# Dealing the second half of the value spread and the state readings out in turn on TensorE, in a hybrid decoder step

## The reference

```
cm_new = decay * cm + w_end * outer(vc, kc)        # state update: decay, then a rank-1 term
num    = ... cm, qc ...                            # the state read by the query
```

## Time and profile before

| | us |
|---|---|
| runs of the kernel before, median of 3 (lowest, highest) | 2174.12 (2170.67, 2176.59) |
| profiled execution | 2170.06 |
| its span, first to last instruction | 2168.2 |
| TensorE matmul busy in the span | 2078.0 (96%) |
| mean granted TensorE clock | 0.957 of full speed |

### The profile page before, as it was taken

The page is one execution under the profiler, slowest core; times in us unless marked ns, Lnnn a source line. Parts: engine busy times, 40 slices in busy tenths (PEclk is TensorE's granted clock), DMA queues, the critical chain, the costliest instruction groups (busy, mean ns, idle before and its releaser), DMA issues.

```text
span 2168.2 us, 39328 instructions
## 1 busy us (share of the span) xinstructions
PE 2078.0 (96%) x16091; PEld 1968.4 (91%) x16091; DVE 1221.4 (56%) x1836; ACT 977.0 (45%) x1594; POOL 285.8 (13%) x288
## 2 busy tenths in 40 slices
PE   7999999998999989999999997999999999999997
PEld 6998878996899979988799976999999999999997
DVE  6556445543556665655355425566566656665665
ACT  4444234444454544441344433454454545454544
POOL 0891122000000007921220000000000000000000
PEclk9999779999999999997799997999999999999999
DMA  7553224458446355532244484454546454545543
GB/s 271 185 173 111 98 86 141 173 190 328 167 154 213 135 194 195 176 110 95 88 138 157 166 328 166 146 195 153 185 148 213 149 194 157 198 151 184 190 157 114
DMA packets 64331, 367.08 MB, mean 169 GB/s; under 512 B 7332, under 2 KB 11876, under 8 KB 32036
## 3 DMA queue, kind: packets, MB, share of 16 engines
q1 hardware_dynamic: 62116, 357.98, 47.5%
q0 software_dynamic: 2048, 6.62, 0.9%
HBM read 340.09 MB, written 24.48 MB: 168 GB/s over the span
## 4 chain that ended last, share of the span: by engine, by line
PE 88%; DMA 5%; DVE 4%; ACT 2%; issue 1%; SPq 0%; DVEq 0%; ACTq 0%
PE ps L535 23%; PE ps L536 23%; PE ps L537 23%; PE ps L745 3%; DMA ring<-w_v_dram 3%; PE ps L759 2%; PE ps L521 2%; DVE wL L315 1%; PE ps L549 1%; DMA ring<-w_o_dram 1%; ACT wH L309 1%; PE ps L552 1%; PE ps L772 1%; PE ps L556 1%; PE ps L551 1%
## 5 line engine op out<-in xcount | busy, mean ns | idle before, releaser
L315 DVE TENSOR_TENSOR wL<-ring,wH 128x1024 fp32r<-128x1024 f32 x591 | 741.4, 1257 | 487.2 <-ACT wH L309 484.5
L535 PE MATMUL ps<-hH,wH 128*128 128x264 f32 x2784 | 802.7, 288 | 20.6 <-DVE wL L315 8.0
L536 PE MATMUL ps<-hL,wH 128*128 128x264 f32 x2784 | 793.8, 285 | 0.0
L537 PE MATMUL ps<-hH,wL 128*128 128x264 f32 x2784 | 793.0, 285 | 0.0
L309 ACT ACTIVATE wH<-ring 128x1024 fp32r<-128x1024 f32 x591 | 621.7, 1055 | 300.4 <-PE ps L537 254.3
L535 PEld LDWEIGHTS ps<-hH,wH 128*128 128x128 f32 x2784 | 529.5, 190 | 31.5 <-issue 21.4
L536 PEld LDWEIGHTS ps<-hL,wH 128*128 128x128 f32 x2784 | 529.9, 190 | 0.5
L537 PEld LDWEIGHTS ps<-hH,wL 128*128 128x128 f32 x2784 | 527.2, 189 | 0.0
L535 PE MATMUL ps<-projR,wH 128*128 128x264 f32 (+1 forms) x1520 | 434.7, 286 | 10.2 <-DVE projR L1656 5.9
L537 PE MATMUL ps<-projR,wL 128*128 128x264 f32 (+1 forms) x1520 | 431.9, 284 | 0.0
L536 PE MATMUL ps<-projR,wH 128*128 128x264 f32 (+1 forms) x1520 | 431.9, 284 | 0.0
(11 more groups left out here) (277 smaller groups left out, 1772.3 us busy)
## 6 DMA issues: line engine op xcount, KB each, us to landing
ring<-w_gu_dram SPq DMA_DIRECT2D x110, 1024.0 KB, 4.9
ring<-w_in_dram SPq DMA_DIRECT2D x58, 1024.0 KB, 4.9
ring<-w_down_dram SPq DMA_DIRECT2D x80, 704.0 KB, 4.1
stream<-states_dram SPq DMA_DIRECT2D x32, 512.0 KB, 4.2
ring<-w_out_dram SPq DMA_DIRECT2D x16, 1024.0 KB, 4.8
o_states_dram<-stream SPq DMA_DIRECT2D x32, 512.0 KB, 4.6
ring<-kc_dram SPq DMA_DIRECT2D x16, 1024.0 KB, 6.8
ring<-vc_dram SPq DMA_DIRECT2D x16, 1024.0 KB, 7.5
```

The lines of the kernel that those rows point to most:

```text
L315: dve.tensor_tensor(wL[:, buf * PIECE:(buf + 1) * PIECE], slot(s, half * PIECE, PIECE), f32(wH[:, buf * PIECE:(buf + 1) * PIECE]), ALU.sub ...
L535: pe.matmul(dst, wh, high(k0 + k), start=k0 + k == 0, stop=False)
L536: pe.matmul(dst, wh, low(k0 + k), start=False, stop=False)
L537: ins = pe.matmul(dst, wl, high(k0 + k), start=False, stop=k0 + k == k_all - 1)
```

## The change

`spread(i + 1)` and `read_out(i)` become three pieces. `spread_first(i + 1)` issues the four matmuls of the first half and raises `dec_bc` as before. `spread_and_read(i)` then deals out the four of the second half and the eight readings: one spread, two readings, four times over. The fourth spread raises `dec_bc`, the eighth reading raises `dec_mv`. The number and the operands of the matmuls are the same. The first unit's spread has no readings beside it, and the last unit's readings (`read_last`) have no spread beside them.

```diff
--- before.py
+++ after.py
@@ -733,19 +733,22 @@
                         ins = pe.matmul(bank(5, 0, P), mKW(h)[:, st * P:(st + 1) * P], mV(h)[:, st * P:(st + 1) * P], start=st == 0, stop=st == 1)
                     ins.then_inc(ret_num, 1)
 
-                def spread(u):
-
-                    v = unit_cols(u)[1]
-                    for hf in range(2):
-                        n = 2 * (l * UNITS + u) + hf
-                        if u:
-                            pe.wait_ge(dec_S, n - 1)
-                        for b in range(NB // 2):
-                            at = hf * (NB // 2) + b
-                            ins = pe.matmul(bank(hf, b * P, P), v[:, at:at + 1].to_broadcast([P, P]), ident, start=True, stop=True)
-                        ins.then_inc(dec_bc, 1)
-
-                def read_out(u):
+                def spread_half(u, hf):
+
+                    n = 2 * (l * UNITS + u) + hf
+                    if u:
+                        pe.wait_ge(dec_S, n - 1)
+                    for b in range(NB // 2):
+                        yield pe.matmul(bank(hf, b * P, P), unit_cols(u)[1][:, hf * (NB // 2) + b:hf * (NB // 2) + b + 1].to_broadcast([P, P]), ident,
+                                        start=True, stop=True)
+
+                def spread_first(u):
+
+                    for ins in spread_half(u, 0):
+                        last = ins
+                    last.then_inc(dec_bc, 1)
+
+                def read_columns(u):
 
                     n, q = l * UNITS + u, unit_cols(u)[2]
                     pe.wait_ge(dec_S, 2 * (n + 1))
@@ -756,8 +759,23 @@
                     elif u < NH + SP:
                         pe.wait_ge(ssd_h, l * SP + u - NH + 1)
                     for b in range(NB):
-                        ins = pe.matmul(bank(read_bank(u), 448 + b, 1), state(u)[:, b * P:(b + 1) * P], q[:, b:b + 1], start=True, stop=True)
-                    ins.then_inc(dec_mv, 1)
+                        yield pe.matmul(bank(read_bank(u), 448 + b, 1), state(u)[:, b * P:(b + 1) * P], q[:, b:b + 1], start=True, stop=True)
+
+                def spread_and_read(u):
+
+                    columns = read_columns(u)
+                    for b, ins in enumerate(spread_half(u + 1, 1)):
+                        if b == NB // 2 - 1:
+                            ins.then_inc(dec_bc, 1)
+                        next(columns)
+                        read = next(columns)
+                    read.then_inc(dec_mv, 1)
+
+                def read_last(u):
+
+                    for ins in read_columns(u):
+                        last = ins
+                    last.then_inc(dec_mv, 1)
 
                 def post_sum(p):
 
@@ -797,7 +815,10 @@
                         first_part(0)
                 evicted(N_PROJ - 2)
                 evicted(N_PROJ - 1)
-                spread(0)
+                spread_first(0)
+                for ins in spread_half(0, 1):
+                    last = ins
+                last.then_inc(dec_bc, 1)
                 for i in range(UNITS):
                     if i + 1 < UNITS:
                         first_part(i + 1)
@@ -810,8 +831,10 @@
                     else:
                         ret_d(i - NH - SP)
                     if i + 1 < UNITS:
-                        spread(i + 1)
-                    read_out(i)
+                        spread_first(i + 1)
+                        spread_and_read(i)
+                    else:
+                        read_last(i)
                 post_sum(POSTS - 2)
 
                 lows = [Q_ML + h for h in range(NH)] + [Z + j for j in range(SP)] + [Q_R + h for h in range(RH)]
```

## The result

The changed kernel takes 2177.47 us (median of 20 runs, 2172.87 to 2184.41), the kernel before, timed between those runs, 2170.36 us (20 runs, 2165.78 to 2177.18). The ratio is 1.0029, with an interval of [1.0019, 1.0040]: 6.3 us more, with bounds of 4.1 and 8.7 (the two medians as they stand differ by 7.1). That is slower without doubt. The ratio itself is just inside the 0.3% that the forecast called no change, the upper bound is not. The forecast was +2.5 us.

The account below looks back on a forecast made before the run. TensorE, busy 96% of the span, was taken as the bound. Terms 0 + 1.5 + 1.0 + 0 = +2.5 us on the 2174.12 us median gave 2176.6, predicted as 2176.5 us; range 2165 to 2186 us.

Parts of the forecast that it names:

- Passes: TensorE's spread and reading passes in 30 units: each switch's saving and cost nearly equal, 0 us in sum.
- hidden loads: Rival: readings' weight loads hide, each added switch to readings saves 0.11 us, time 2167 us; chance 0.07.
- a price for each return to a spread: Rival: each TensorE change from one-column to 128-column matmul costs 0.10 us, 9.0 us over 90, time 2186 us; chance 0.15.
- Second half later: VectorE's second half of the update is late, lengthening TensorE's idle time before L772 by 0.75 us, twice: +1.5 us.
- First readings of the SSD units: TensorE's earlier first reading waits for VectorE's L1607, 0.08 us, twelve times: +1.0 us, bounds 0 and 2.4.
- The clock: Half clock in four mLSTM and SSD stretches loses 58 us; the new order was taken to change it by 0.
- the rival by which the clock falls a little more often: Readings dilute the wide spreads that lift the clock; a tenth more of 58 us, +5.8, time 2182 us; chance 0.05.
- The rival by which the clock stays up: Thinned-out readings keep the mixers' clock up; one fifth of 58 us returns, 12 us, time 2165 us; chance 0.12.
- two dips: TensorE's clock was read as full except near slices 4 to 6 and 18 to 20 of 40, the mixers.
- a gap-free stretch that loses the clock: In an mLSTM unit, TensorE was busy for all 3.3 us at half clock, so being busy did not keep the clock.
- The observables: Signs: dealt SSD stretch 3.4 to 3.6 us, second half detached, L772 idle 1.4 us, four stretches' clocks within 0.02.

Follow-up runs that it names:

- the mLSTM experiment: Dealt order in the six mLSTM units of each layer only, order of before elsewhere, against the kernel before: 2174.77 us, ratio 1.0008.
- The late signal alone: Kernel before with its TensorE order kept; only the second half's dec_bc increment raised by the sixth reading instead of the eighth spread: 2173.70 us, ratio 1.0003.
- SSD alone: Dealt order in the six SSD units of each layer only, order of before elsewhere, against the kernel before: 2179.78 us, ratio 1.0027.
- where the waits are gone: Only SSD units dealt, readings starting one spread later and last spread behind two readings, against the kernel before: 2174.26 us, ratio 1.0004.
- full rows: Kernel before with operands of causal matmuls L549, L551 and L632 padded from 6 or 12 to 128 partitions: 2086.62 us, ratio 0.9598.
- the wide work put between the two: Kernel before with mLSTM's transposes and scores moved between the readings and the causal matmuls: 2161.30 us, ratio 0.9943.

## Why the prediction held, and where it was 4 us short

The time itself, 2177.47 us against the 2176.5 predicted, is closer than the forecast of the change, and that is luck: the prediction stood on the median of three runs of the kernel before, 2174.12 us, and 20 runs have 2170.36.

**Passes, taken at 0: right.** mLSTM and retention units keep their 3.57 and 3.47 us to 0.01 us, and the mLSTM experiment is at 1.0008. The two rivals on passes, hidden loads and a price for each return to a spread, are both refuted: each would have moved every mLSTM unit, by 0.3 us or more. The saving and the cost of a switch cancel, as the two rows of before had said.

**Second half later, taken at +1.5 us: right.** The forecast had the wait at `post_sum` grow from 0.68 to 1.43 us, twice; it is 1.37, so +1.4 us. The late signal alone gives 1.27. VectorE's waits before the second half of the update, 0.93 to 1.29 us where the readings are those of an SSD or retention unit and none where they are an mLSTM unit's, came as said, and in the retention units none of it reached TensorE.

**First readings of the SSD units, taken at 0.08 us each: the term that was mis-sized.** It is 0.24 us in each of the 8 units that begin at full clock, 1.9 us in the profiled execution instead of 1.0. It lies over the bound of 0.2 us per unit, too. The prediction had counted from the end of L1607 to the moment at which the reading wants to go. What counts is the start of its weight load, which stands 0.11 us ahead of the first pass (343.36 and 343.47), and what lies between an instruction's end on VectorE and the load that it releases was left out: 344.60 to 344.72, 0.12 us, and the same in all 8 units. The two together make the 0.24 us. Of the 4 units that begin at half clock, one (at 1063.98, where the clock is back after the first pass) has the long first group of readings too, 0.58 us; with it the term is some 2.1 us. In the other three the first group takes 0.34 to 0.38 us: the slower spreads cover most of the wait. The 4 take 3.67 to 3.83 us from first record to last, and such units of before 3.67 to 4.02.

**The clock, taken at 0: about 2 us, not shown beyond doubt.** The two waits sum to 2.1 + 1.4 = 3.5 us; the full-clock part grew by 2.4 ± 0.5 (3.4 in the kernel with SSD alone). The lost part grew by 2.4 ± 1.1 over one chip's runs of the kernel before, by 1.6 ± 0.9 over the other's; by 3.2 ± 1.1 for SSD alone, and by 0.7 ± 1.1 where the waits are gone. Both parts together are 4.8 or 4.2 us, not 6.3: the 20 runs of the kernel before beside the changed one have a mean of 2171.3 us, the two sets of 23 runs 2173.1 and 2173.6. So some 2 us of the 6.3 are placed in neither part. The growth of the lost part agrees with the rival by which the clock falls a little more often, at about a third of its price. It goes with the two waits, but the late signal has one of them and loses nothing (-1.1 ± 0.8). The rival by which the clock stays up is refuted: nothing near the 9 us from which it would have decided.

Two readings of the prediction on the clock were wrong and did not enter the sum. It called L549 to L552 six rows in the array; L550 and L552, half of them, have 128 rows. And it saw two dips, where the slice at 1301 us has 0.7 as well.

On the clock the Trainium skill, "TensorE: Matmul & The Clock Gate", advises against idle gaps of TensorE as what lets the clock fall. The trace of before had it at 0.50 through 3.3 us without a gap, and full rows now show the converse: the same matmuls and the same readings, only with 116 or 122 more partitions that add nothing to the sums, and 1.00 throughout the same stage. What the prediction said of a gap-free stretch that loses the clock has held; that the rows in the array were the larger lever, next to which the order was worth little, it had not seen.

**The observables.** Two of four held: the detached second half, and `post_sum` at 1.4. The dealt stretch did not: 3.71 us in SSD units is over the 3.4 to 3.6 named, and at 0.24 us off 3.47 it is past the 0.2 us from which the prediction was to count as wrong. That sign is the mis-sized term above. The mean clock moved by some 0.001 over the runs, against the 0.004 named. The clocks of the four stretches did not all stay within 0.02 (0.87 instead of 0.80 in layer 1's first), which was a poor test, as the falls lie elsewhere in each execution; over whole mixers they moved by -0.01 and +0.02.

## What to carry to other kernels

When an instruction that waits is moved forward, its price is counted from the releaser's end plus the time that the release takes (0.12 us here), against the moment at which its weight load would start, and a slack of 0.1 us is no slack: one spread more ahead of the first reading, and the last spread behind two readings instead of six, made the change free. Interleaving two kinds of matmul whose passes take the same time, as the one-column and the 128-column ones here, changed nothing by itself on thin rows (ratio 1.0008); on full rows it went with a loss of clock whose cause is open. Where the clock is below full while TensorE is busy, look at how many rows its operands fill before looking at the order: padding them with zeros gave 86 us here, a better order 12, and the change studied -6.

## What the runs showed of the hardware that had not been expected

Operands of 6 or 12 partitions cost twice. First, they slow themselves and the passes around them: at full clock two passes of L551 with 6 rows take 0.41 us, and two of their neighbour L552 over 128 columns with 128 rows 0.42, while among full-row ones each pair takes 0.22. Of the chain of waits of before, beside the earlier trace rows:

```profile
227.93 0.41 PE ps L551 x2
```

This is the spacing of the passes, and the length of a record doesn't tell it: L551's records at full clock last 270 ns with few rows and 275 with 128.

The Trainium skill, "TensorE: Matmul & The Clock Gate", step-by-step part on LDWEIGHTS, has the load's time depend on the columns and not on the rows. The trace of before agrees for the load itself: its records last at least 180 ns with 6 rows (L551) and 186 with 128 (L552). Yet with few rows the spacing of the passes was nearly twice the 0.112 us that full rows have, so the number of rows does matter where it changes from one matmul to the next. Why it does, no run here separates.

Second, the low clock of the mixers hangs on them: 59 of the 96 us that the half clock takes go away with full rows, with all the single-column readings still in place. That the readings beside them have a part in it is seen from the wide work put between the two, which brought 16.7 us back. Whether it is the rows themselves or the wider spacing of the passes that lowers the clock was not tested.

And the same change costs more on a faster stage: dealing costs 6.3 us on thin rows and 13.7 on full ones, where the readings come sooner against VectorE's work, and where 6.6 us are a loss of clock that neither theory had expected.
